# Streaming encoder step with a grouped mixture of experts: some expert weights in pieces, and the last two experts reordered

## The reference

```
for e in range(16):
    h = silu(t @ w_gate[e]) * (t @ w_up[e])      # 1024 -> 512, twice
    y = y + gate[:, e:e + 1] * (h @ w_down[e])   # 512 -> 1024
x = layernorm(ALPHA * x + y, ln2_g, ln2_b)
```

## Time and profile before

| | |
|---|---|
| median of 3 runs | 916.42 us (915.0 to 918.24) |
| profiled execution: span | 916.5 us |
| TensorE matmuls busy | 793.1 us (87%) |
| VectorE busy | 335.0 us (37%) |
| ScalarE busy | 187.3 us (20%) |
| bytes moved by DMA | 272.8 MB, mean 298 GB/s |

### The profile page before, as it was taken

The page is one execution under the profiler, slowest core; times in us unless marked ns, Lnnn a source line. Parts: engine busy times, 40 slices in busy tenths (PEclk is TensorE's granted clock), DMA queues, the critical chain, the costliest instruction groups (busy, mean ns, idle before and its releaser), DMA issues.

```text
span 916.5 us, 9955 instructions
## 1 busy us (share of the span) xinstructions
PE 793.1 (87%) x3943; PEld 387.2 (42%) x3943; DVE 335.0 (37%) x749; ACT 187.3 (20%) x452; POOL 44.0 (5%) x58
## 2 busy tenths in 40 slices
PE   6978999998899886876879989979898999777875
PEld 4665777453433222222334567654534333222221
DVE  1016455445422212122281054654533442122138
ACT  1213343110321101110110025620103211111101
POOL 1012000003000000000100000000020000000020
PEclk9998899899999999998989999999989999999998
DMA  9724007736999999999799060581679999999991
GB/s 357 232 72 196 1 1 297 300 153 239 402 424 423 425 428 422 425 426 424 265 350 361 3 261 1 215 330 53 275 282 424 431 423 429 422 428 423 428 398 57
DMA packets 43552, 272.80 MB, mean 298 GB/s; under 512 B 6360, under 2 KB 11166, under 8 KB 25840
## 3 DMA queue, kind: packets, MB, share of 16 engines
q1 hardware_dynamic: 32032, 243.69, 64.6%
q0 software_dynamic: 5888, 19.95, 6.5%
q10 hardware_dynamic: 5584, 8.51, 2.6%
HBM read 253.92 MB, written 18.21 MB: 297 GB/s over the span
## 4 chain that ended last, share of the span: by engine, by line
PE 56%; DMA 25%; DVE 9%; SPq 6%; ACT 2%; issue 1%; ACTq 0%; DVEq 0%
DMA arena<-in_expert_w_up 24%; PE bank L916 16%; PE bank L858 6%; PE bank L930 5%; PE bank L1176 5%; PE bank L845 3%; SPq L502 2%; PE bank L832 2%; PE bank L777 2%; PE bank L939 2%; PE bank L1049 2%; PE bank L825 1%; PE bank L679 1%; PE bank L1141 1%; PE bank L868 1%
## 5 line engine op out<-in xcount | busy, mean ns | idle before, releaser
L916 PE MATMUL bank<-arena 128*64 128x512 f32 x1024 | 240.7, 627 | 48.2 <-DMA arena<-in_expert_w_up 46.5
L916 PEld LDWEIGHTS bank<-arena 128*64 128x64 f32 x1024 | 77.2, 144 | 208.4 <-issue 148.8
L930 PE MATMUL bank<-arena 128*64 128x512 f32 x512 | 116.9, 598 | 16.7 <-DVE arena L1825 16.7
L1825 DVE COPY arena<-bank 128x256 f32<-128x256 f32 x32 | 13.6, 424 | 271.8 <-PE bank L923 271.8
L930 PEld LDWEIGHTS bank<-arena 128*64 128x64 f32 x512 | 34.1, 136 | 77.4 <-issue 54.6
L1378 ACT ACTIVATE arena<-bank 128x256 f32<-128x256 f32 x32 | 12.3, 384 | 265.8 <-PE bank L916 265.8
L1833 DVE RECIPROCAL arena<-arena 128x256 f32<-128x256 f32 x32 | 56.1, 1753 | 1.1
L858 PE MATMUL bank<-arena 128*128 128x512 f32 x128 | 56.0, 595 | 0.0
L1176 PE MATMUL bank<-arena 128*128 128x512 f32 x96 | 43.9, 619 | 6.6 <-ACT arena L1483 5.7
L1234 ACT COPY arena<-bank 128x512 f32<-128x512 f32 (+2 forms) x30 | 15.8, 537 | 112.9 <-PE bank L679 74.2
L858 PEld LDWEIGHTS bank<-arena 128*128 128x128 f32 x128 | 24.0, 190 | 29.6 <-issue 29.5
(11 more groups left out here) (272 smaller groups left out, 870.1 us busy)
## 6 DMA issues: line engine op xcount, KB each, us to landing
arena<-in_expert_w_gate SPq DMA_DIRECT2D x32, 2048.0 KB, 20.6
arena<-in_expert_w_up SPq DMA_DIRECT2D x32, 2048.0 KB, 25.6
arena<-in_expert_w_down SPq DMA_DIRECT2D x64, 1024.0 KB, 27.9
arena<-in_w_out SPq DMA_DIRECT2D x4, 2048.0 KB, 9.5
expert_rows<-arena ACTq DMA_DIRECT2D x60, 128.0 KB, 7.9
arena<-in_w_kv_shared SPq DMA_DIRECT2D x3, 2048.0 KB, 10.5
arena<-in_w_mem_kv SPq DMA_DIRECT2D x2, 2048.0 KB, 21.1
arena<-sorted_rows POOLq DMA_DIRECT2D x2, 2048.0 KB, 9.2
```

Of the source, the lines that this page charges most:

```text
L916: last = mm(bank[j][64 * half:64 * half + 64, :].rearrange("p (u f) -> p u f", u=2), slots[:, k, 0:CAP], w[:, :, k, 256 * half:256 * half ...
L930: last = mm(bank[3 + j][64 * n:64 * n + 64, :], hid_t[:, j, c, 64 * half:64 * half + 64], w[:, half, c, 512 * n:512 * n + 512], start=(hal ...
```

## The change

It has two parts.

First, up weights of experts 3, 4 and 15 come in four pieces of two chunks `k` each. A piece is one transfer for gate and one for up, 512 KB each, and has its own semaphore. For the buffer of expert e+3, TensorE's up stage of e (0, 1 and 12) now signals `part_done` after its chunks 2, 4 and 6, and SyncE issues each piece when its part of the buffer is free. TensorE waits for each piece ahead of the first chunk that needs it. The other experts have one piece, as before.

Second, the last experts change order. On TensorE it was up 15, down 14, down 15; it becomes down 14, up 15, down 15. ScalarE copies out 14 ahead of the exponential of 15, and SyncE issues the down weights of 14 (which wait for down 11) ahead of the up weights of 15 (which wait for up 12). VectorE's program is the same.

```diff
+        def pieces(e):
+            return 4 if e in (3, 4, NE - 1) else 1
+        def piece_loads(l, e, i):
+            return 32 * sum((m, f) <= (l, e) and f % 3 == e % 3 and pieces(f) > i for m in range(DEPTH) for f in range(NE))
+        def marks(e):
+            return sorted({KC * (i + 1) // pieces(e + 3) for i in range(pieces(e + 3) - 1)}) if e + 3 < NE else []
...
-            for e in range(3, NE):
+            for e in range(3, NE - 1):
                 yield "up", e
                 yield "down", e - 1
+            yield "down", NE - 2
+            yield "up", NE - 1
             yield "down", NE - 1
+        def load_order():
...
+            for e in range(3, NE - 4):
+                yield "up", e
+                yield "down", e - 1
+            yield "down", NE - 5
+            yield "up", NE - 4
+            yield "down", NE - 4
...
-            def load_up(l, e, buffer, s):
+            def load_up(l, e, buffer, s, k0=0, k1=KC):
                 for u, name in enumerate(("expert_w_gate", "expert_w_up")):
                     src = ins[name][l][bass.ds(e, 1)].rearrange("o (p k) f -> (o p) k f", k=KC)
-                    sp.dma_start(buffer[:, u], src).then_inc(s, 16)
+                    sp.dma_start(buffer[:, u, k0:k1], src[:, k0:k1]).then_inc(s, 16)
+            def load_next_up(l, e):
+                n = pieces(e + 3)
+                for i in range(n):
+                    if i < n - 1:
+                        sp.wait_ge(part_done, parts(l, e, i))
+                    else:
+                        sp.wait_ge(up_done, NE * l + e + 1)
+                    load_up(l, e + 3, ups[e % 3], up_in[e % 3][i], KC * i // n, KC * (i + 1) // n)
...
-            def expert_up(j, w, slots):
+            def expert_up(j, w, slots, arrivals=(), leaves=()):
+                arrivals = dict(arrivals)
                 for k in range(KC):
+                    if k in arrivals:
+                        pe.wait_ge(*arrivals[k])
                     for half in range(2):
                         last = mm(...)
+                    if k + 1 in leaves:
+                        last.then_inc(part_done, 1)
                 return last
...
-                    gate(e)
-                    if e + 2 < NE:
-                        take(e + 2)
-                    (keep if PAIR[l] and e == NE - 1 else store)(e - 1)
+                    if e < NE - 1:
+                        gate(e)
+                        if e + 2 < NE:
+                            take(e + 2)
+                        store(e - 1)
+                    else:
+                        (keep if PAIR[l] else store)(e - 1)
+                        gate(e)
```

More of the change, by code:

```diff
@@ L287, in encoder_step @@
         w_in = {n: sem("w_" + n) for n in ("mem0", "mem1", "ina", "uq", "ukv", "out0", "kvs0", "kvs1", "kvs2", "inb", "out1")}
-        up_in = [sem(f"up_in{b}") for b in range(3)]
+        up_in = [[sem(f"up_in{b}_{i}") for i in range(4)] for b in range(3)]
         dn_in = [sem(f"dn_in{j}") for j in range(3)]
@@ L312, in encoder_step @@
         rows_turned = sem("rows_turned"); rows_taken = {"a": sem("rows_taken_act"), "v": sem("rows_taken_dve")}
-        xg_ready = sem("xg_ready"); up_done = sem("up_done"); sig_ready = sem("sig_ready"); h_ready = sem("h_ready")
+        xg_ready = sem("xg_ready"); up_done = sem("up_done"); part_done = sem("part_done"); sig_ready = sem("sig_ready"); h_ready = sem("h_ready")
         ht_ready = sem("ht_ready"); ht_copied = sem("ht_copied"); down_done = sem("down_done"); y_copied = sem("y_copied")
@@ L405, in loads, with parts @@
             return l * len(range(e % 3, NE, 3)) + e // 3 + 1
+        def pieces(e):
[4 more added lines that the diff above has]
+            return sorted({KC * (i + 1) // pieces(e + 3) for i in range(pieces(e + 3) - 1)}) if e + 3 < NE else []
+        def parts(l, e, i):
+            return sum(len(marks(f)) for m in range(l) for f in range(NE)) + sum(len(marks(f)) for f in range(e)) + i + 1
         def stores(l, e):
@@ L433, in expert_order @@
             yield "up", 2
-            for e in range(3, NE):
+            for e in range(3, NE - 1):
                 yield "up", e
                 yield "down", e - 1
+            yield "down", NE - 2
+            yield "up", NE - 1
             yield "down", NE - 1
+        def load_order():
+            yield "up", 0
+            yield "up", 1
+            yield "down", 0
+            yield "down", 1
+            yield "up", 2
+            for e in range(3, NE - 4):
[4 more added lines that the diff above has]
+            yield "down", NE - 4
         ROW_BLOCKS = [(P * b, min(P, PACK - P * b)) for b in range(-(-PACK // P))]
@@ L537, in experts @@
                 sp.wait_ge(proj_ready, job_end(before_gu0))
-                load_up(l, 0, ups[0], up_in[0])
+                load_up(l, 0, ups[0], up_in[0][0])
                 if before_down != before_gu0:
@@ L546, in experts @@
                 sp.wait_ge(o_ready, sum(NS[:l + 1]))
-                load_up(l, 1, ups[1], up_in[1])
+                load_up(l, 1, ups[1], up_in[1][0])
                 if l == 1:
@@ L550, in experts @@
                 sp.wait_ge(proj_ready, job_end(before_gu1))
-                load_up(l, 2, ups[2], up_in[2])
+                load_up(l, 2, ups[2], up_in[2][0])
                 load_down(l, 2, 2, dn_in[2])
[L553 to L557, removed]
+                for what, e in load_order():
+                    if what == "up":
+                        load_next_up(l, e)
+                    else:
                         sp.wait_ge(down_done, NE * l + e + 1)
@@ L963, in up @@
                 def up(e):
-                    pe.wait_ge(up_in[e % 3], 32 * loads(l, e))
+                    n = pieces(e)
+                    arrivals = [(KC * i // n, (up_in[e % 3][i], piece_loads(l, e, i))) for i in range(n)]
                     if e < 2:
@@ L970, in up @@
                         pe.wait_ge(xg_ready, (NE - 2) * l + e - 1)
-                    expert_up(e % 2, ups[e % 3], xg[:, e % 2]).then_inc(up_done, 1)
+                    expert_up(e % 2, ups[e % 3], xg[:, e % 2], arrivals, marks(e)).then_inc(up_done, 1)
                 def down(e):
```

## The result

The changed kernel took 927.44 us (median of 9 runs, 919.57 up), the kernel before 916.51 us (9 runs): ratio 1.0078, interval 1.0054 to 1.0102. A second measurement of the same kernel gave 920.5 against 917.18 us, ratio 1.0041 (1.0016 to 1.0066). I forecast 912.4 us and gave "slower" a chance of 0.10. One run of the nine, at 1356 us with a mean granted clock of 0.556, is left out of the ratio; the median of the other eight is 924.3 us. One figure of the prediction was wrong from the start: the time of an execution is 1.7 to 1.9 us more than the span of its profile (928.65 us against 926.8 after, 918.24 against 916.5 before), so the time of the first profile was 918.2 and not 916.5 us; against the miss this is small.

A forecast was written before the change was run, and what follows sets the result against it. The experts were taken as bound by the bytes of one DMA queue. Start and end gains of 0.3 + 1.4 + 0.8 + 1.6 = 4.1 us took 916.5 to 912.4 us, with an 8-in-10 range of 909 to 916.

The forecast's parts named there:

- The bound: Both expert stages: limited by the bytes of one DMA queue, not by TensorE or VectorE.
- the plateau: DMA throughput of 422 to 431 GB/s in slices 11 to 19 and 30 to 38, nearly all of both expert stages.
- The start, 0.3 + 0.8 us: Experts 3 and 4: earlier pieces fill 1.4 and 1.9 us (layers 0, 1), small packets cost 1.1 us in each layer.
- The hollow at 680 to 684: Layer 1 start: windows at 279 and 170 GB/s, short of 425, room for 0.80 MB or 1.9 us.
- I cost that at nothing: Expert start: pieces delay the sorted rows, free because these are turned only behind down 0, over 18 us after up 0 begins.
- The end of layer 0, 1.4 us: Layer 0: down 15 starts 3.0 us sooner, ends 1.3 us sooner, memory projection likewise; taken as 1.4, bounds 1.1 and 3.0.
- the hole: TensorE idle 3.5 us between up 15 and turn 15; the half clock then costs down 15 1.7 us.
- The base of 9.9 us: Expert 15's up weights: time for 4.19 MB at 425 GB/s, before 0.5 us for small packets.
- The end of layer 1, 1.6 us: Layer 1: turn 15 comes 2.0 us sooner on VectorE's chain, 1.6 us left after the wait for sums; bounds 0.9 and 2.5.
- The clock stays up: Rival: no half clock in the TensorE pauses at both stage ends, tail gains 2.6 and 2.0, 910.8 us; chance 0.15.
- The start gives nothing: Rival: sorted rows and pieces trade places, packets cost 1.1 us in each layer, 915.7 us, no visible change; chance 0.20.
- Small transfers cost too much: Rival: each of 18 extra pieces has a price, 923 us at 0.6 us each, 957 us at 2.5; slower, chance 0.10.

The follow-up runs named there:

- experiment 1: Only the new order of the last two experts, all up weights in one piece, against the kernel before: ratio 1.0171 (1.0143 to 1.0199).
- profile a: Another single profile of the kernel before, no edit: 227.9 us from down 15 to up 0 of layer 1, 696.1 us from up 0 of layer 0 to the end.
- start_only: Only experts 3 and 4 in four pieces, expert 15 whole, old order, against the kernel before: ratio 1.0083 (1.0052 to 1.0113).
- experiments 5: The whole change plus three matmuls on constants between up 15 and turn 15, against the kernel before: ratio 1.0023 (0.9982 to 1.0063).
- 11: The kernel before with six matmuls on constants in place of four ahead of the router's ranks, against the kernel before: ratio 0.9997 (0.9958 to 1.0036).
- 12: New order, expert 15 in two pieces, matmuls on constants: four before turn 15, one before the memory projection, six at the router; against the kernel before: ratio 1.0011.
- experiments 7: New order, expert 15 in two pieces, experts 3 and 4 whole, matmuls on constants before turn 15, against the kernel before: ratio 0.9986 (0.9944 to 1.0027).

## Why the prediction was wrong

**The bound.** Right: the plateau is there after as before, and nothing of the change alters it. (Two labels are off by one: the first up stage that waits, at 320.10 in rows 7, is up 8 with the count from 0, and the slices over 420 GB/s begin with the 12th and the 31st.)

**The start, 0.3 + 0.8 us.** The balance was right in kind and too hopeful. At up 15 the early start is worth 0.4 and 0.5 us, not 1.4 and 1.9; the packets cost 0.3 and 1.5 us, not 1.1 each. Together this is nothing in layer 0 and a loss of 1.0 us in layer 1, where I had a gain of 0.3 and 0.8. The hollow at 680 to 684 was not all free room: with the pieces in the queue the tail of the sorted rows runs at 328 and 299 GB/s. And "I cost that at nothing" for the sorted rows was wrong in layer 0: they were issued 3.0 us after up 0, the second of their two transfers took 18.6 us to land, and TensorE waited 3.90 us for them. It was hidden: up 9 to 14 still waited for their weights, 2.1 to 3.7 us each.

**The end of layer 0, 1.4 us.** This is the step that failed first. Down 15 was to start 3.0 us sooner and, with 1.7 us for the hole, to end 1.3 us sooner; counted from the sorted rows it starts 1.4 us sooner (217.8 against 219.2 us) and ends 1.0 us later (223.8 against 222.9). So the stage misses the forecast by 2.3 us, in two terms.

The first 1.6 us are missing ahead of down 15. The last piece of up 15 landed 211.1 us after the sorted rows where the forecast had 436.2 - 226.2 = 210.0: down 14's weights came 0.5 us later than forecast, and the 4 MB behind them took 11.0 and not 10.4 us. The base of 9.9 us was too short, since the 425 GB/s of the plateau are not the weights' alone: in experiment 1, without any pieces, the same 4 MB took 10.5 us. The packets' 0.54 us fits this profile; the other two of the changed kernel have 11.4 us. The last quarter of up 15 took 1.94 and not 1.74 us, and the turn, in the half clock, 0.2 us more.

The other 0.7 us are the charge of the hole. The hole was 3.51 us as computed, but down 15 lost 2.4 us and not 1.7. That charge had been read from one course of the clock; in profile a of the kernel before up stages after idle times of 3.7 and 3.8 us took 9.9 to 10.0 us, 2.8 to 2.9 more than at the full clock, and up 15 after 3.05 us took 7.09 and lost nothing. Filling the hole gave 2.7 us back in the stage, so its cost is shown; with the old order, and so without the hole, four pieces of expert 15 end the stage 5.2 us sooner than the whole change (218.7 against 223.8).

I ended the account there. Up 0 of layer 1 is 2.0 + 2.3 = 4.3 us later, counted from up 0 of layer 0. Of the 2.0 us 1.1 are the sorted rows of layer 0, issued 3.0 and not 1.9 us behind up 0. The 2.3 us, with the 1.7 us on the memory projection (15.67 against 13.97 us) in them, are not shown to be the hole's: filling it did not remove them, and profile a has them to 0.1 us.

**The end of layer 1, 1.6 us.** Turn 15 came sooner as forecast, 899.53 - 683.34 = 216.2 us after the sorted rows were issued where it was 891.51 - 673.09 = 218.4. The 2.2 us were then lost to three things. Down 15's weights held it up for 1.34 us: expert 15 in pieces took 10.8 us in the full queue (883.2 to 894.0; 10.4 in experiment 1 without pieces, 9.9 in the forecast), and the down weights behind it another 7.2 us for 2 MB (5.5 before), while the gather, started 206.7 us after the sorted rows in place of 210.0, used the engines too; that it was the gather was not tested. The half clock cost 6.43 - 3.65 = 2.8 us on down 15, where I had 1.7. So down 15 ended 1.4 us later than before, where I had it 0.3 us sooner, and the last wait of the chain is now VectorE's 1.48 us for TensorE's sums. From the sorted rows to the end it is 243.5 us against 243.4: nothing gained, where start and end of layer 1 were to give 2.4 us.

**What I didn't account for.** From up 0 of layer 1 to the end 2.9 us more, although the stretch from the sorted rows is equal: the rows are issued 1.25 us behind up 0 and no longer 1.57 ahead of it, 2.8 us, and the whole bound stage counts from the rows. That follows the course of the clock at the router. Profile a shows the kernel before with it, 3.9 us slower than its other course. Against profile a only the stage of layer 0 is longer in the changed kernel, by 2.2 to 3.5 us; for the rest of the loss no run shows that the edit is its cause.

**The sum.** From up 0 of layer 0 the profiles give 699.4, 699.3 and 698.0 us against 692.2, 692.4 and 696.1: means of 698.9 and 693.6, 5.3 us or 0.6% of the whole, between the two measured ratios of 0.8% and 0.4%. Of the rivals none was the case as it was told. "The clock stays up" was wrong in both layers. "The start gives nothing" was right on its own, but left the tails as gains. "Small transfers cost too much" ended on the right side for a wrong reason: a piece cost some 0.1 us (four took 0.4 to 0.9 us more than the whole), and SyncE was held up by them,

```profile
853.20 7.75 SPq L560 DMA_DIRECT2D arena<-in_expert_w_gate  x1
861.00 4.23 SPq L560 DMA_DIRECT2D arena<-in_expert_w_up  x1
```

7.75 and 4.23 us where an issue takes 0.33 to 0.44 us (in the full queue of the kernel before some took 1.3 to 3.1 us too), but the queue behind it never ran dry (over 400 GB/s in every window of 2 us from 866 to 902).

The rule of the Trainium skill ("TensorE: Matmul & The Clock Gate", Part 1) that an idle TensorE has to work its way up again fits the hole made and the hole filled: down 15 took 6.0 us with it and 3.65 us without. It did not give the price of a single pause, as the 3.05 us that cost nothing in profile a show. I used it for one hole and one stage; what followed the stage was left out.

**Open.** Why the course of the clock differs between executions of one kernel, in the memory projection and at the router, and whether the edit brings the slower one on. Also the time ahead of up 0 in layer 0, 218.4 to 228.5 us: it spreads more than the effect under study and was not taken apart. The 1.0083 of `start_only` stays without a mechanism.

## What to carry to other kernels

Bringing the last load in pieces pays when something still lies between the last matmul that needs it and the next stage: here down 14 did, and taking it away cost more than the pieces gave. Before moving a filler, name what TensorE does in the latency that it covered, and follow a half clock until TensorE has been busy again, past the end of the stage. And anchor a bound stage to what it counts from (here the sorted rows) before comparing two profiles; spans alone mixed 3 to 10 us of other things into this one. The best kernels here, two or four pieces in the old order, gained 2.6 to 4.2 us in each expert stage against the first profile before, and their times could not be told from no change. One profile of each kernel would have hidden why: the second and third profile of the unchanged kernel showed that about half of the 7.2 us under study need no edit.

## What the runs showed of the hardware

- The granted clock followed one of a few courses that repeat closely: in the three profiles of the whole change the half clock lies 6 to 9, 26 to 33, 156 to 163, 200 to 210 and 217 to 221 us behind down 15 of layer 0, and profile a of the kernel before has the same. The two other profiles of the kernel before have it at 23 to 30, 153 (or 156) to 160 and 211 to 221 us. With matmuls on constants added (experiments 5, 11, 12) dips lay elsewhere or were as before, and none of these profiles is free of them.
- The same idle time did not always cost the same: 3.05 us ahead of up 15 cost nothing in profile a of the kernel before, 2.49 us ahead of up 14 of layer 1 cost 1.7 us in the first profile, and the hole of 3.51 us cost 2.4 us on down 15 in layer 0 and 2.8 us in layer 1.
- With nine or more earlier transfers under way an issue on SyncE took up to 3.1 us in the experts of the kernel before, and up to 7.75 us in those of the changed one; others took 0.43 us with as many. At the end of layer 1 the queue stayed full meanwhile.
- In the full queue of the new order the 4 MB of expert 15 took 10.8 to 11.4 us in four pieces (4 KB per partition), 10.5 us in two, and 10.4 to 10.5 us whole (experiments 7 and 1).
- Two streams of 4 KB packets shared the DMA engines about evenly: in 235 to 240 us of layer 0 the sorted rows had 53.3% and the pieces 46.5% of them, and the first 2 MB of rows landed after 15.4 us in place of 9.3.
